# First tile in halves, last tiles by token halves, and three reorderings between them, in a two-block transformer kernel

## The chip, the cores and the metric

One core of a Trainium2 chip runs the kernel. The metric is the device time in microseconds (us) of one launch. TensorE (PE) multiplies, VectorE (DVE) and ScalarE (ACT) work on tiles element by element, GpSimd (POOL) does additions and products, and SyncE (SP) issues every DMA. All tiles are fp32, 128 partitions wide.

## The reference, cut to what matters

Two transformer blocks over 512 tokens of width 1024, then a norm. Cut to what this change touches:

```
# block 1                          # block 2 (same ending, other weights)
u  = rmsnorm(x, g_mix) @ w_in      h = rmsnorm(x1, ln1) @ w_in2   # x1 = rmsnorm(block 1's x, g_fin)
...recurrence, attention...        o_gla  = gated linear attention, o_att = softmax(lse of 3 groups) mix of 12 heads
x += merged @ w_out                mix = (sig(g)*(o_gla*silu(hr))@w_o_gla + sig(g')*o_att@w_o_attn) @ w_out2
x += relu(rmsnorm(x)@w_ff1)**2 @ w_ff2      (the same with w_ml1, w_ml2)
x += sigmoid(rmsnorm(x)@w_pg) * (p@w_ple)   (the same with w_pg2, p_2@w_pp)
                                   y = rmsnorm(x, ln_f)
```

Block 2's first norm is a norm of a norm, so it needs two sums over the width of the squares of block 1's x: a plain one ("n4") and one weighted by g_fin squared ("n5"). The head mix of block 2's attention is a softmax over three group weights for each of 4 heads.

## The kernel before

**Matmuls.** Activations lie transposed, width on partitions, 512 tokens on columns, in 8 row blocks. A weight tile is 128 output columns by 1024 inputs (512 KB). SP loads it into one of 4 buffers RAW, ACT rounds it to fp32r (`whi`, L1106, WHI), DVE makes the remainder (`wlo`, L1658, WLO), in 3 buffers each. A product takes 3 matmuls of 512 columns for each of 8 inner blocks k (`row`, L547 to L549): hi by hi, hi by lo, lo by hi. There are 303 tiles. The activations are split in the same way (`hi` L1137 on ACT, `lo` L1671 or L1669 on DVE).

**Order.** Each engine runs one program in order. It steps through generators woven after one list of rows (`weave_order`); a dense row is the 3 matmuls of one k, so a full tile is 8 rows. The other streams' steps stand ahead of the dense row at which they are put. `due` says at which row of which tile each engine splits or loads a coming tile: ACT at k = 1, DVE at k = 3, SP at k = 5. `lead2(n, skew)` interleaves the rows of a stage's first two tiles.

**Start.** SP loads x block 0, the vectors, weight tile 0, blocks 1 to 3, tile 1, blocks 4 to 7, tile 2, constants, tile 3. Ahead of all weaving, ACT splits the blocks and tiles 0 and 1, then squares 8 blocks (L1121), in turn with POOL's 7 additions (L2323), with two or three buffers between them. Only then does it come to tile 2.

**Norms.** `total` (L568) sums squares over partitions with two ones-matmuls, `norm_rs` takes Ln (L1130) and Exp (L1132) to get RS. An activation function that isn't in the table set that ScalarE holds is preceded by a table load.

**Block 1's gate (pg), then block 2's embedding (emb2).** Per tile i: DVE scales the bank by RS (L1651), ACT sigmoid (L1212), POOL product (L2320), DVE addition into x (L1654), ACT `hi` and square, DVE `lo`, DVE's term of n5 (L1791), POOL's term of n4 (L2323). Both sums take the square as soon as ACT has it. The gate tiles use banks 0 to 3 in turn, and so do the 8 short products of emb2 (2 rows each), which ACT copies out (L1330). Then come n4 and n5, one 16-row tile "ha" and the gla tiles on banks 0 and 1.

**hr stage.** 8 tiles on banks 0 and 1: DVE scales (L1651), ACT sigmoid (L1243), POOL product, DVE product (L1834), ACT hi, DVE lo. In the same rows stream "l" makes the heads' weights on 4 partitions: at row 27 of the stage maximum and difference (L2278), at row 33 two additions, a reciprocal (L2286), a product and three `lo` in one step, and at rows 50, 54, 58 and 62 the mix: 3 small matmuls (L1089) and DVE products each. The stage has 64 rows; the merge of block 2 follows.

**Last gate (pg2) and the end.** Tiles 0 to 6 whole, tile 7 in two token halves of 256 columns. For each half, DVE, ACT, DVE, DVE, ACT (squares L1294, product with ln_f L1296), PE (sums, plain fp32, L649 and L650), ACT (L1300, L1303) and then 8 products (6 on DVE L1651, 2 on POOL) and the stores follow each other.

Of the kernel before, what the change touches and what calls it, by code (L numbers as in the profile page):

```python
# [233 lines left out]
def core_steps():  # L234
# [21 lines left out]
def weave_order():  # L256
# [27 lines left out]
    put("n", A_EMB2 + 8, A_EMB2 + 14, A_HA, *range(A_GL + 1, A_GL + 33, 4))  # L284
# [4 lines left out]
    for n in range(12):  # L289
# [4 lines left out]
    put("l", A_HR + 20, A_HR + 20, A_HR + 20, A_HR + 27, A_HR + 33, *[A_HR + r for r in (50, 54, 58, 62) for _ in range(3)],  # L294
        A_HR + 67)
# [6 lines left out]
def build_kernel(nc, A):  # L302
    ctx = ExitStack()
    with ctx:
# [235 lines left out]
        def tensor_program(e):  # L540
# [31 lines left out]
            def dense():  # L572
# [34 lines left out]
                yield from embed("emb2", T_EMB2, HP2, "HP2")  # L607
# [3 lines left out]
                yield from units(("hr",), T_HR, plain(8), H1, hx("HX2"), ev("hr"), (0, 1))  # L611
# [24 lines left out]
                for half in range(2):  # L636
                    cs = slice(256 * half, 256 * half + 256)
                    b = 4 + half
                    w.wait_ge(D.dve.at("wlo", T_PG2 + 7), free.get(b))
                    for k in range(8):  # L640
                        d = row(bank(b)[:, 0:256], T_PG2 + 7, k, (H3[k][0][:, cs], H3[k][1][:, cs]), k == 0, k == 7)
                        if k == 7:
                            d.then_inc(*D.pe.sig("pg2", 7, half))
                        yield
                for half in range(2):
                    cs = slice(256 * half, 256 * half + 256)
                    acc, tmps = NORM["n8"]
# [2239 lines left out]
```

## Time and profile before

| | us |
|---|---|
| median of 3 runs (lowest, highest) | 2111.76 (2111.15, 2112.51) |
| profiled execution, its own time | 2110.7 |
| its span, first to last instruction | 2108.8 |
| PE busy in it | 2033.7 (96%) |
| DVE, ACT, POOL busy | 990.4, 781.4, 292.6 |

PE is busy for 96% of the span. Its idle time is 75 us, and the profile says for each piece which instruction ended it. The mean granted clock of PE is 0.981 of full speed. Busy times on PE overlap (a matmul is pipelined), so the pace is read from start to start.

### The profile page before, as it was taken

Reading aid. Unit: us, or ns where it says so; the run is one execution under the profiler, and the core shown is the slowest. Engines: PE = TensorE matmul, PEld = TensorE weight load, DVE = VectorE, ACT = ScalarE, POOL = GpSimd, SP = SyncE. Lnnn points to the kernel's source line nnn. Section 1 sums busy time; section 2 is a strip of 40 time slices with the busy share of each in tenths; the row PEclk is TensorE's granted clock in tenths of the full one; section 3 lists DMA queues with packets and bytes.
Section 4 is the critical chain, followed back from the end, with each engine's and each line's share of the span. In section 5 each row is a group of like instructions: output and inputs, shape, how many; then the busy total and the mean of one; then the engine's idle time right before and its main releaser. Section 6 shows DMA issues by size and latency. Waiting matters only on the chain.

```text
span 2108.8 us, 27562 instructions
## 1 busy us (share of the span) xinstructions
PE 2033.7 (96%) x11518; PEld 1629.0 (77%) x11518; DVE 990.4 (47%) x1534; ACT 781.4 (37%) x1233; POOL 292.6 (14%) x292
## 2 busy tenths in 40 slices
PE   7998999999999999999899999998999999999996
PEld 5766767777888778888677788886788888888884
DVE  5665554544553233336855444446643432333354
ACT  5573221223444333234524243335322343322344
POOL 2001121210221001012300000001310220100124
PEclk9999998999999999999999999998999999999997
DMA  5121111111633332322421222221232233322221
GB/s 181 55 70 61 45 48 42 46 47 51 220 100 103 107 103 95 100 93 95 143 90 52 69 71 80 80 90 60 80 100 92 98 125 106 100 98 97 96 80 50
DMA packets 59843, 185.46 MB, mean 88 GB/s; under 512 B 6551, under 2 KB 11799, under 8 KB 59592
## 3 DMA queue, kind: packets, MB, share of 16 engines
q1 hardware_dynamic: 59720, 183.71, 26.2%
q8 instruction: 91, 1.49, 0.3%
q14 instruction: 32, 0.26, 0.0%
HBM read 173.46 MB, written 10.22 MB: 87 GB/s over the span
## 4 chain that ended last, share of the span: by engine, by line
PE 87%; DVE 4%; ACT 4%; issue 2%; POOL 1%; DMA 1%; SPq 0%; DVEq 0%; POOLq 0%; ACTq 0%
PE P L547 25%; PE P L549 24%; PE P L548 24%; DVE AREN L1651 1%; PE P L822 1%; PE P L858 1%; PE P L912 1%; PE P L851 1%; PE P L910 1%; PE P L807 1%; DVE WLO L1658 1%; POOL AREN L2323 1%; DVE AREN L1654 1%; PE P L1035 1%; DVE AREN L1791 1%
## 5 line engine op out<-in xcount | busy, mean ns | idle before, releaser
L547 PE MATMUL P<-HH,WHI 128*128 128x512 f32 x1528 | 624.6, 409 | 22.4 <-DVE WLO L1658 12.2
L549 PE MATMUL P<-HH,WLO 128*128 128x512 f32 x1528 | 603.7, 395 | 0.0
L548 PE MATMUL P<-HL,WHI 128*128 128x512 f32 x1528 | 602.8, 394 | 0.0
L1106 ACT ACTIVATE WHI<-RAW 128x1024 fp32r<-128x1024 f32 x303 | 318.9, 1053 | 443.9 <-PE P L549 440.8
L1658 DVE TENSOR_TENSOR WLO<-RAW,WHI 128x1024 fp32r<-128x1024 f32 x303 | 381.7, 1261 | 150.1 <-ACT WHI L1106 148.8
L547 PEld LDWEIGHTS P<-HH,WHI 128*128 128x128 f32 x1528 | 291.0, 190 | 100.4 <-issue 15.4
L547 PE MATMUL P<-ARR,WHI 128*128 128x512 f32 (+1 forms) x904 | 351.7, 389 | 7.6 <-DVE AREN L1651 2.9
L549 PE MATMUL P<-ARR,WLO 128*128 128x512 f32 (+1 forms) x904 | 350.1, 387 | 0.0
L548 PE MATMUL P<-ARR,WHI 128*128 128x512 f32 (+1 forms) x904 | 350.1, 387 | 0.0
L549 PEld LDWEIGHTS P<-HH,WLO 128*128 128x128 f32 x1528 | 291.1, 190 | 63.3
L548 PEld LDWEIGHTS P<-HL,WHI 128*128 128x128 f32 x1528 | 291.4, 191 | 55.9 <-issue 0.2
L2320 POOL TENSOR_TENSOR AREN<-AREN 128x512 f32<-128x512 f32 (+1 forms) x126 | 132.8, 1060 | 1155.8 <-ACT AREN L1351 560.1
L547 PEld LDWEIGHTS P<-ARR,WHI 128*128 128x128 f32 x904 | 169.7, 188 | 48.1 <-DVE WLO L1658 5.0
L1651 DVE TENSOR_TENSOR AREN<-P,RS 128x512 f32<-128x512 f32 (+1 forms) x136 | 102.2, 752 | 217.0 <-PE P L549 200.6
L549 PEld LDWEIGHTS P<-ARR,WLO 128*128 128x128 f32 x904 | 169.7, 188 | 34.6
L548 PEld LDWEIGHTS P<-ARR,WHI 128*128 128x128 f32 x904 | 169.8, 188 | 34.5
L2323 POOL TENSOR_TENSOR AREN<-AREN 128x512 f32<-128x512 f32 x75 | 117.3, 1564 | 454.6 <-DVE AREN L1651 198.8
L1654 DVE TENSOR_TENSOR AREN<-AREN,P 128x256 f32<-128x256 f32 (+2 forms) x168 | 81.1, 496 | 194.6 <-PE P L549 149.9
L1940 DVE TENSOR_TENSOR ARR<-AREN,ARR 128x512 fp32r<-128x512 f32 x64 | 44.3, 692 | 227.7 <-POOL AREN L2320 211.2
L1351 ACT ACTIVATE AREN<-P 128x512 f32<-128x512 f32 x64 | 38.2, 597 | 200.5 <-PE P L549 200.5
L1651 DVE TENSOR_TENSOR AREN<-AREN 128x256 f32<-128x256 f32 (+1 forms) x80 | 43.3, 560 | 55.8 <-ACT AREN L1402 18.4
L1651 DVE TENSOR_TENSOR AREN<-P,CST 128x256 f32<-128x256 f32 (+3 forms) x80 | 34.4, 447 | 65.8 <-PE P L822 31.5
(297 smaller groups left out, 1553.1 us busy)
## 6 DMA issues: line engine op xcount, KB each, us to landing
RAW<-in_w_in_dram SPq DMA_DIRECT2D x118, 512.0 KB, 3.3
RAW<-in_w_ff_dram SPq DMA_DIRECT2D x64, 512.0 KB, 3.3
RAW<-in_w_ml_dram SPq DMA_DIRECT2D x64, 512.0 KB, 3.2
RAW<-in_w_out_dram SPq DMA_DIRECT2D x16, 512.0 KB, 3.3
RAW<-in_w_pg_dram SPq DMA_DIRECT2D x16, 512.0 KB, 3.3
AREN<-in_xT_dram SPq DMA_DIRECT2D x16, 256.0 KB, 6.4
s_gates<-AREN SPq DMA_DIRECT2D x16, 256.0 KB, 2.0
RAW<-in_w_ab_dram SPq DMA_DIRECT2D x8, 512.0 KB, 3.4
```

The source lines that it names most:

```text
L547: e.matmul(out, hi, H[0][:, s], start=first, stop=False)
L548: e.matmul(out, hi, H[1][:, s], start=False, stop=False)
L549: return e.matmul(out, lo, H[0][:, s], start=False, stop=last)
L807: d = e.matmul(v3(o, 4)[:, 2 * j + p, :], BK[rws[h], j, 2 * p:2 * p + 2, :], AR[rws[h], j, :, p, :], start=True, stop=True)
L1106: e.activation(WHI[n % NSPL][:, :], RAW[n % NRAW][:, :], ACT.Copy).then_inc(*D.act.sig("whi", n))
L1351: e.activation(r, bank((0, 1, 2, 3)[j % 4]), ACT.Relu).then_inc(*D.act.sig(H1, q, j))
L1651: return e.tensor_tensor(out, a, b, ALU.mult)
L1654: return e.tensor_tensor(out, a, b, ALU.add)
L1658: e.tensor_tensor(WLO[n % NSPL][:, :], RAW[n % NRAW][:, :], WHI[n % NSPL][:, :].bitcast(F32), ALU.subtract).then_inc(*D.dve.sig("wlo", n))
L1940: e.tensor_tensor(HD[j][1], ar(19 + u % 3), HD[j][0].bitcast(F32), ALU.subtract).then_inc(*D.dve.sig(f + "D", q, j))
L2320: return e.tensor_tensor(out, a, b, ALU.mult)
L2323: return e.tensor_tensor(out, a, b, ALU.add)
```

## The change

1. *Start.* SP loads the first 512 columns of tile 0 ahead of x block 0, the rest after block 3, tile 1 after block 5, tiles 2 and 3 ahead of the constants; ACT and DVE split tile 0 in two halves. POOL first zeroes a buffer, on which PE runs three plain fp32 matmuls. The first two tiles are interleaved with a skew of 6 rows instead of 2. Of n1's squares, two stay ahead of the weaving and six move into it; POOL adds the first four and DVE the rest; the total goes to bank 2; lambda's small work moves to tiles 3 and 4.
2. *Table sets.* `norm_hi` of n2, n3, n6 and n7 loads the table set that has both Ln and Exp.
3. *n4 and n5.* In the pg stage DVE adds n4 itself; n5's terms (`second`) move to emb2's rows. Squares stay in buffers 30 to 37. emb2 uses banks 4 to 7 and 0 to 3. n4's total is at row 2 of ha (bank 4) and n5's at row 6 (bank 5), instead of row 14 of emb2 and row 0 of ha.
4. *hr.* Four banks instead of two. The weights' steps are at rows 25, 31, 37, 43 and 49, the reciprocal in two halves; the mix is at rows 56, 68, 80 and 92, the last three of which lie in the merge.
5. *End.* Tiles 0 to 4 whole; then tiles 5, 6, 7 for tokens 0 to 255 and again for tokens 256 to 511, so that half 0's sum, its RS and the product of its first 4 blocks on POOL come among half 1's rows. Tile 7's squares are on DVE. The results are written as 4-, 3- and 2-block products on DVE.

```diff
+def last_rows():
+    yield from lead2(5, 0)
+    for u in range(6):
+        for k in range(8):
+            yield 5 + u, k
+def last_steps(j, k):
+    at = {(0, 7): "evac", (1, 0): "sigmoid", (1, 1): "mult", (1, 2): "add", (1, 3): "square", (1, 4): "sum"}
+    return [(5 + u % 3, u // 3, at[j - 5 - u, k]) for u in range(6) if (j - 5 - u, k) in at]
...
-    put("n", A_EMB2 + 8, A_EMB2 + 14, A_HA, *range(A_GL + 1, A_GL + 33, 4))
+    put("n", A_EMB2 + 14, A_HA + 2, A_HA + 6, *range(A_GL + 1, A_GL + 33, 4))
...
-    put("l", A_HR + 20, A_HR + 20, A_HR + 20, A_HR + 27, A_HR + 33, *[A_HR + r for r in (50, 54, 58, 62) for _ in range(3)],
-        A_HR + 67)
+    put("l", A_HR + 20, A_HR + 20, A_HR + 20, *range(A_HR + 25, A_HR + 50, 6),
+        *[A_HR + r for r in (56, 68, 80, 92) for _ in range(3)], A_HR + 97)
...
-                g = units(("attn",), T_AT, lead2(12, 2), H1, hx("HX"), ev("attn"), (0, 1, 6, 7))
+                w.wait_ge(K.pool.at("zero"))
+                for _ in range(3):
+                    e.matmul(bank(3), ar(52)[:, 0:128], ar(52), start=True, stop=True)
+                g = units(("attn",), T_AT, lead2(12, 6), H1, hx("HX"), ev("attn"), (0, 1, 6, 7))
...
-                yield from embed("emb2", T_EMB2, HP2, "HP2")
+                yield from embed("emb2", T_EMB2, HP2, "HP2", (4, 5, 6, 7, 0, 1, 2, 3))
-                yield from units(("hr",), T_HR, plain(8), H1, hx("HX2"), ev("hr"), (0, 1))
+                yield from units(("hr",), T_HR, plain(8), H1, hx("HX2"), ev("hr"), (0, 1, 2, 3))
...
+                for half, banks in ((0, (4, 5, 6)), (1, (1, 2, 3))):
+                    cs = slice(256 * half, 256 * half + 256)
+                    for t, b in zip((5, 6, 7), banks):
+                        w.wait_ge(D.dve.at("wlo", T_PG2 + t), free.get(b))
+                        for k in range(8):
+                            d = row(bank(b)[:, 0:256], T_PG2 + t, k, (H3[k][0][:, cs], H3[k][1][:, cs]), k == 0, k == 7)
+                            if k == 7:
+                                d.then_inc(*D.pe.sig("pg2", t, half))
+                                if half and t == 5:
+                                    last_total(0, 7)
+                            yield
+                last_total(1, 0)
...
             def norm_hi(N_):
+                if N_ not in ("n4", "n5"):
+                    e.preload_act_table_set("natural_log_exp_and_others")
...
                         if at == "lo":
                             lo("HX2", i, hblk(i), xs, g=gl[:, i:i + 1])
-                            w.wait_ge(N.act.at("sq", "n4", i), K.pool.at("gf2"), N.dve.at("n5", i - 1))
...
+                            if i:
+                                w.wait_ge(N.act.at("sq", "n4", i), N.dve.at("n4", i - 1) if i > 1 else None)
+                                add(ar(3), ar(30 if i == 1 else 3), ar(30 + i)).then_inc(*N.dve.sig("n4", i))
+                    for i in [k // 2] if j == 8 and k % 2 == 0 else [4] if (j, k) == (8, 7) else []:
+                        second(i)
...
                 for k in range(8, 16):
                     embed_row(T_EMB2, k)
+                    if k < 11:
+                        second(k - 3)
...
-                e.reciprocal(dZ, dZ).then_inc(*L.dve.sig("zr"))
-                w.wait_ge(L.dve.at("zr"))
+                for half in range(2):
+                    cs = slice(256 * half, 256 * half + 256)
+                    e.reciprocal(dZ[:, cs], dZ[:, cs]).then_inc(*L.dve.sig("zr", half))
+                    yield
+                w.wait_ge(L.dve.at("zr", 1))
                 mul(dL, dL, dZ.unsqueeze(1).to_broadcast([4, 3, 512])).then_inc(*L.dve.sig("lw"))
+                yield
...
             def begin():
+                name, i = TILES[0]
+                load("first", 0, RAW[0][:, 0:512], A[name][i, :, 0:512])
                 for j in range(8):
...
-                    if j in (0, 3, 7):
-                        weights((0, 3, 7).index(j))
+                    if j == 5:
+                        weights(1)
+                    if j == 3:
+                        load("raw0", 0, RAW[0][:, 512:1024], A[name][i, :, 512:1024])
+                weights(2)
+                weights(3)
                 load("cst", 0, CST[:, :], A["consts"])
```

## Rows read from the trace of the kernel before

**Rows 1.** Waits of PE: who waited, for whom: us in total, times, longest.

```profile
PE P L547 <- DVE WLO L1658: 15.1, 8, 9.4
PE P L649 <- ACT AREN L1294: 13.3, 2, 8.0
```

**Rows 2.** Timeline of the start: start, us, engine, line, operation [idle before <-releaser].

```profile
7.00 1.06 ACT L1106 ACTIVATE WHI<-RAW 128x1024 fp32r<-128x1024 f32 x1 [2.33 <-DMA RAW<-in_w_in_dram]
...
9.37 0.80 PE L547 MATMUL P<-HH,WHI 128*128 128x512 f32 x1 [9.37 <-DVE WLO L1658]
...
10.87 1.06 ACT L1106 ACTIVATE WHI<-RAW 128x1024 fp32r<-128x1024 f32 x1 [0.57 <-DMA RAW<-in_w_in_dram]
...
12.10 0.63 PE L547 MATMUL P<-HH,WHI 128*128 128x512 f32 x1
...
12.52 0.63 PE L548 MATMUL P<-HL,WHI 128*128 128x512 f32 x1
...
14.69 0.43 PE L547 MATMUL P<-HH,WHI 128*128 128x512 f32 x1
...
15.50 10.86 POOL L2323 TENSOR_TENSOR AREN<-AREN 128x512 f32<-128x512 f32 x7 [10.82 <-ACT AREN L1121]
...
25.27 0.50 PE L547 MATMUL P<-HH,WHI 128*128 128x512 f32 x1 [2.21 <-DVE WLO L1658]
...
32.35 0.47 PE L547 MATMUL P<-HH,WHI 128*128 128x512 f32 x1 [0.87 <-ACT RS L1130]
```

**Rows 3.** Timeline from gate to gla: PE, DVE, ACT.

```profile
995.48 1.28 ACT L1132 ACT_TABLE_LOAD   x1
...
999.39 0.50 PE L547 MATMUL P<-ARR,WHI 128*128 128x512 f32 x1 [0.46 <-DVE WLO L1658]
...
1020.75 2.31 DVE L1658 TENSOR_TENSOR WLO<-RAW,WHI 128x1024 fp32r<-128x1024 f32 x1
...
1025.45 1.78 DVE L1791 SCALAR_TENSOR_TENSOR AREN<-AREN,GF 128x512 f32<-128x512 f32 x1
...
1030.86 0.75 DVE L1671 SCALAR_TENSOR_TENSOR HL<-AREN,DVC,HH 128x512 fp32r<-128x512 f32 x1 [0.19 <-ACT HH L1137]
...
1036.79 0.50 PE L547 MATMUL P<-ARR,WHI 128*128 128x512 f32 x1 [2.90 <-DVE AREN L1651]
...
1056.16 0.47 PE L547 MATMUL P<-HH,WHI 128*128 128x512 f32 x1 [1.61 <-DVE AREN L1651]
```

**Rows 4.** Timeline of hr: DVE, PE.

```profile
1456.56 3.34 DVE L2286 RECIPROCAL AREN<-AREN 4x512 f32<-4x512 f32 x1
...
1462.51 0.39 PE L549 MATMUL P<-HH,WLO 128*128 128x512 f32 x1
...
1470.60 0.77 PE L547 MATMUL P<-HH,WHI 128*128 128x512 f32 x1 [7.71 <-DVE AREN L1651]
...
1483.63 0.50 PE L547 MATMUL P<-HH,WHI 128*128 128x512 f32 x1
```

**Rows 5.** Stretch of 10 us in hr: us, busy (x) of PE, PEld, DVE, ACT, POOL, PE clock, DMA.

```profile
1470.00:1480.00 10.00, 9.40 (x21) 6.56 (x22) 8.07 (x10) 2.85 (x5) 5.14 (x4) 0.50 0.22 61
```

**Rows 6.** Timeline of the end.

```profile
2058.93 1.76 DVE L1654 TENSOR_TENSOR AREN<-AREN 128x512 f32<-128x512 f32 x1 [1.18 <-POOL AREN L2320]
...
2065.05 0.39 PE L547 MATMUL P<-ARR,WHI 128*128 128x512 f32 x1
...
2065.73 0.39 PE L547 MATMUL P<-ARR,WHI 128*128 128x512 f32 x1
...
2083.61 0.28 PE L549 MATMUL P<-ARR,WLO 128*128 128x256 f32 x1
...
2085.76 0.42 DVE L1651 TENSOR_TENSOR AREN<-P,RS 128x256 f32<-128x256 f32 x1
...
2099.22 1.22 PE L649 MATMUL P<-AREN,CST 128*128 128x256 f32 x2 [7.99 <-ACT AREN L1294]
...
2102.29 3.16 DVE L1651 TENSOR_TENSOR AREN<-AREN 128x256 f32<-128x256 f32 x6 [3.93 <-ACT AREN L1303]
```

More of the change, by code:

```diff
@@ L635, in dense, with last_total @@
                     yield
-                for half in range(2):
+                for half, banks in ((0, (4, 5, 6)), (1, (1, 2, 3))):
                     cs = slice(256 * half, 256 * half + 256)
[L638 to L647, printed above, removed]
-                    w.wait_ge(N.pool.at("add", "n8", 6), N.act.at("sq", "n8", 7 + half), free.get(6 + half))
-                    e.matmul(bank(6 + half)[:, 0:256], cst("ones"), ar(acc)[:, cs], start=True, stop=False)
-                    e.matmul(bank(6 + half)[:, 0:256], cst("ones"), ar(tmps[(7 + half) % 2])[:, cs], start=False,
-                             stop=True).then_inc(*N.pe.sig("sum", "n8", half))
+                    for t, b in zip((5, 6, 7), banks):
[8 more added lines that the diff above has]
+                last_total(1, 0)
+            def last_total(half, b):
+                cs = slice(256 * half, 256 * half + 256)
+                acc, tmps = NORM["n8"]
+                w.wait_ge(N.pool.at("add", "n8", 6, half), K.pool.at("one"), free.get(b))
+                e.matmul(bank(b)[:, 0:256], cst("ones"), ar(acc)[:, cs], start=True, stop=False)
+                w.wait_ge(N.dve.at("sq", "n8", 7, half))
+                e.matmul(bank(b)[:, 0:256], cst("ones"), ar(tmps[1])[:, cs], start=False,
+                         stop=True).then_inc(*N.pe.sig("sum", "n8", half))
             def block(t_out, out, HM_, hm, emb, t_emb, HP_, hp, f, t_ml, n2, pg, t_pg, n3, h3):
@@ L1305, in whi_mg2, with last_rs @@
+            def last_rs(half, b):
+                rs = ar(6)[:, 256 * half:256 * half + 256]
+                w.wait_ge(N.pe.at("sum", "n8", half))
+                e.activation(rs, bank(b)[:, 0:256], ACT.Ln, scale=1.0 / 1024, bias=EPS6).then_inc(
+                    *N.act.sig("ln", "n8", half))
+                w.wait_ge(N.act.at("ln", "n8", half))
+                e.activation(rs, rs, ACT.Exp, scale=-0.5).then_inc(*N.act.sig("rs", "n8", half))
             def whi_mg2(i, k):
@@ L2511, in dilated @@
                         yield
-                for _ in range(5):
+                for _ in range(8):
                     yield
```

287 lines of the change are left out of this document (170 added, 117 removed).

## The prediction

> **What bounds the kernel now.** I read PE's waits first. The two longest kinds, 15.1 us for `wlo` and 13.3 us for ScalarE's squares [rows 1], lie with few others in five stretches; outside them PE is fed without a break, and a row of three matmuls takes 0.68 us from start to start (2065.05 to 2065.73) [rows 6], a tile 5.44 us. So only what shortens an idle stretch of PE, or the work behind its last matmul, is worth anything. Then I read the timeline of each stretch. In the start the reader is to see that PE begins at 9.37, that its matmuls come 0.42 us apart (12.10, 12.52) until 14.69, and that ScalarE's and GpSimd's alternation on n1 (10.86 us) keeps tile 2 from being split [rows 2]. From gate to gla, that VectorE is what PE waits for [rows 3]. In hr, that one scaling behind the reciprocal stops PE, and that the clock is at half for some 13 us behind the stop [rows 4, 5]. At the end, that 25 us follow PE's last tile [rows 6].
>
> **Part 1, the start.** Before, 16 rows of the first two tiles, tile 2 (24 matmuls) and n1's total end such that tile 3 starts at 32.35 [rows 2]. After: tile 0 landed by 7.00, when 0.85 MB were issued ahead of and with it; tile 1 by 10.87, at 2.16 MB; that is 340 KB per us [rows 2]. In the new order tile 1 ends at 2.68 MB, so it lands near 10.87 + 0.52/0.34 = 12.4. Blocks 6 and 7 follow, 0.26 MB each: 13.2 and 14.0. With ACT's split of tile 1 (1.06), VectorE's (1.2), then `hi` (0.7) and `lo` (0.75 [rows 3]), row 6 can start near 15.2. The six rows of tile 0 ahead of it (8 us at the slow pace, from near 7) fit before. The ten left are 6.8 us: both tiles end at 22. Tile 2 is split by then, since only two squares stand before it (ACT free near 16, split at 18). It takes 5.44, the total 0.5, and the total's bank no longer holds tile 3 (0.87 [rows 2]): tile 3 starts near 28.3 instead of 32.35. Gain 4.0. The three plain fp32 matmuls lie before the first load has landed; if they cost more than that, up to 1 us of row 0, it is before the data-bound rows. Bounds: 6.8 us of the ten rows become 12.8 where they run at the slow pace, gain -2; tile 1 landing at 11, gain 5.4.
>
> **Part 2, the table sets.** In pg and pg2 a table load of 1.28 stands between Ln and Exp [rows 3], and one ahead of Ln: RS comes some 2.5 us sooner. Tile 3 then doesn't wait (0.46 and 0.3 of refilling the pipe [rows 3]): 0.75 in each of the two stages, counted in parts 3 and 5. In the two MLPs no wait hangs on RS: 0.
>
> **Part 3, gate to gla.** From tile 3's start at 999.39 to gla's at 1056.16 [rows 3] there are 196 matmuls (5 tiles 120, emb2 48, totals 4, ha 24), 44.4 us at the full pace; 56.8 were taken. VectorE per gate tile had `wlo` 2.31, `lo` 0.75, n5's term 1.78, addition and scaling 0.68 each: 6.2 us against 5.44. The 2.31 (elsewhere 1.23) and the 1.78 (0.75 for the like `lo`) overlap with GpSimd's additions of n4 [rows 3]. After it: 1.23 + 0.75 + 4 x 0.68 less one, 4.0, and at most 1.1 for GpSimd's product (an addition of 0.68 took 1.76 beside one [rows 6]): 5.1, under PE's 5.44. So the gate tiles run at PE's pace, and end at 998.65 + 27.2 = 1025.9. Eight banks take away the waits of emb2 (2.90 for the last scaling [rows 3], 1.8 for the copies): it ends at 1036.8. What is late next is n4. The scaling of tile 7 comes some 2.5 us behind PE at 1028.4, as the chain from RS through product and addition to the next scaling lags; behind it stand on VectorE the rest of the last two tiles, eight terms of n5 and two `wlo`, 12.4 us: n4's `lo` ends near 1041. PE is at ha's row 2 at 1038.2 and waits 2.7. Four rows and the second total later it is 1044.6, then product 0.7, Ln and Exp 1.4, RS 0.7 and ha's scaling 0.7 (bank 0, which gla's first tile needs): gla starts at 1048.1. Gain 56.16 - 48.1 = 8.0, the 0.75 of part 2 in it. Bounds: no wait left but ha's, 10.5; n5's terms at 1.78 instead of 0.75, which is 8 us more of VectorE, 1.5. I take 8.0, as GpSimd has nothing to do in emb2's rows.
>
> **Part 4, hr.** PE's fifth tile ends at 1462.74 (the last start is 1462.51), the next starts at 1470.60; from there to 1483.63 are 18 matmuls and two mix groups [rows 4], at half clock (0.50 [rows 5]). At full pace these are 18 x 0.2265 + 2 x 1.8 = 7.7 us of the 13.0. The stop and the slow clock cost 7.9 + 5.3 = 13.2. After: VectorE's chain in these rows doesn't get shorter, but two scalings more may be late. I count it from the end T of tile 2 (1446.4 before): difference 4.9, `wlo` and product 6.7; additions and half a reciprocal (3.34/2 [rows 4]) 9.8; tile 3 scaled 11.1; `wlo`, the other half, product, `lo`, tile 4 scaled 16.9; product of the weights and `wlo` of tile 7 19.9; tile 5 scaled 22.7; the weights' three `lo` 23.3, 24.0, 24.6. PE needs bank 3 at T + 27 and `wlo` of tile 7 at T + 21.8: no wait. But the mix at row 56 comes at T + 21.8 and wants the weights at 23.3 to 24.6: PE idles some 1.9, and a stop of 2.90 left the next matmuls at their full pace in part 3's stretch, so no clock is lost. The nine other mix products lie beside the merge, whose first need for the mix is row 112, 15 rows (10 us) behind the last step. Gain 13.2 - 2.2 = 11.0. Bounds: each of the four long VectorE steps 1.1 later for GpSimd's product, with the clock falling again, 5; no wait, 13.2.
>
> **Part 5, the end.** Before, tile 7 ends at 2083.9 and the span at 2108.8 [rows 6]. After, tiles 0 to 4 end at 2066.3 (0.75 sooner). Each half tile is 24 matmuls of 0.12: 2.9 us. Half 0 ends at 2075, half 1's tile 5 at 2077.8. VectorE lags here too (it scales tile 7's half 0 at 2085.76, 4.9 us behind PE [rows 6]); with RS 2.5 sooner, tile 5 half 0 is scaled near 2072.7, and each half tile takes scaling 0.42, sigmoid 0.4, product 0.45, addition 0.42, square and product 0.8, 2.3 to 2.5 in all: tile 7's square on VectorE ends at 2079.8. PE waits 1.5 for it, the sum ends at 2080.35, half 1's tiles end at 2083.2 and 2086.1. RS of half 0 is at 2081.3, then a table load 1.28 ahead of tile 5's sigmoid at 2082.6. GpSimd's product of 1024 columns takes some 2.6 (2 x 1.3) from there; VectorE's product of tile 5 is behind it and comes at 2084.4. From there each half tile is 2.3 again: last addition 2089.2, square 2089.6, PE 2090.2 to 2090.7 (slow), Ln and Exp 2091.6, results 0.9, 0.9 and 0.7: 2094.1, and 3.3 for the last store, as before (2102.29 + 3.16 to 2108.8): 2097.3. Gain 11.5. Bounds: a lag as large as before and all contended operations at 1.76 instead of 0.68 (some four on the chain), 7; half 1 free of GpSimd and PE's clock full, 13.
>
> A row first: VectorE's addition beside GpSimd's product took 1.76 instead of 0.68 [rows 6], that is, about to the end of that product. The Trainium skill (SBUF — State Buffer, "Who interferes with whom") says that the two share a port pair which one holds for a whole instruction, and that the other fully blocks. By that the one long product on GpSimd can hold VectorE for its whole 2.6 us, where four short ones would let it in between: it speaks against this piece of the change, the end would be near 2098.5, and the total 1.2 later.
>
> **Sum.** 4.0 + 8.0 + 11.0 + 11.5 = 34.5 us. The profiled execution took 2110.7 for a span of 2108.8; the median is 2111.8, 1.1 above. 2111.8 - 34.5 = 2077.3; I say 2078.
>
> **Rivals.**
> *A, the weights come later than PE in hr.* VectorE is in order, and four long steps stand among its eight tiles; for it speaks that it was busy 8.1 of 10 us there [rows 5], against it that four banks give 16 us of slack. PE would stop some 6 us at row 56, with a slow clock behind it: gain there 3, total 2086.
> *B, the end keeps its length.* The half tiles' chain lags as tile 7 did; PE then waits 4 us for half 0's sum and the rest moves with it: gain 7, total 2082.
> *C, the start runs at the slow clock.* PE has pauses between the first six rows, where it had none: gain -2 in part 1, total 2084.
> *D, the other side: the slow clock lasts.* Rows are 1.28 us at half clock, tiles 10.2 instead of 5.44 [rows 2, 6], 4.8 us lost each. A start with pauses, or the pause in hr, would have to hold it for 8 tiles (35 + 4 us) for the kernel to be slower by over 0.2%; at nine it is 2120. Against it: the clock was back some 5 us after 9.37 and 13 us after 1470.60.
> *E, nothing changes.* It would need VectorE's load in emb2's rows and in hr to give all back; no row says so.
>
> **Chances and range.** My forecast, within 4 us: 45%; A 17%, B 14%, C 11%, a better one (all stops gone, 2071) 9%, D 3%, E 1%. The range 2070 to 2089 takes in A to C with their neighbours and leaves out some 15%. A difference of 0.2%, 4.2 us, is about what can be told from none: faster 0.95, same 0.02, slower 0.03.
>
> **What would show it.** Tile 3 starts near 28 and no wait for `wlo` near 22; fp32 matmuls before the first load. Between gate and gla, `wlo` at 1.23, one wait of 2 to 3 us for n4's `lo` and one of 2 for ha's scaling. In hr one wait below 3 us ahead of the mix and a clock of 1.00. At the end less than 12 us between PE's last fp32r matmul and the last instruction. A wait of over 3 us ahead of the mix, or ahead of half 0's sum, or matmuls 0.42 us apart for most of the first 25 us, proves me wrong there.

## The result and the profile after

The changed kernel takes 2089.73 us (median of four executions, 2086.41 to 2093.19), the kernel before on the same chip 2111.45 (2109.63 to 2112.51): a ratio of 0.9911, 95% interval 0.9885 to 0.9937. It is 21.7 us faster. The prediction was 2078 with a range of 2070 to 2089, so the time lies 0.7 us outside it, which is less than the 6.8 us by which the four executions differ. The direction was right, and more than a third of the forecast gain is missing.

The profiled execution took 2090.74 for a span of 2089.0 (before 2110.7 and 2108.8). To see where the time went I cut both spans at the same weight tiles: a stage lasts from the start of VectorE's `wlo` of one tile to that of another, so a stage means the same work in every kernel. The cuts after are at 60.21, 952.17, 1110.21, 1393.03, 1550.64 and 2033.12.

| us | before | after | gained | predicted |
|---|---|---|---|---|
| start | 64.60 | 60.21 | 4.4 | 4.0 |
| recurrence and first half of block 1 | 892.40 | 891.96 | 0.4 | 0 |
| gate to gla | 159.69 | 158.04 | 1.65 | 8.0 |
| dil | 282.80 | 282.82 | 0.0 | 0 |
| hr and merge | 161.26 | 157.61 | 3.65 | 11.0 |
| out2 and second MLP | 482.48 | 482.48 | 0.0 | 0 |
| end | 65.57 | 55.88 | 9.7 | 11.5 |

Start and end came as forecast or nearly so; of the 19 us forecast for the two stages in the middle, 5.3 arrived. The waits of PE, which for the kernel before were led by 15.1 and 13.3 us for `wlo` and the squares [rows 1], now read so (who waited, for whom: us in total, times, longest):

```profile
PE P L1116 <- DVE ARR L2396: 5.9, 2, 5.7
PE P L675 <- POOL AREN L2428: 4.3, 2, 2.5
...
PE P L561 <- ACT AREN L1382: 2.6, 1, 2.6
...
PE P L561 <- DVE WLO L1712: 1.8, 1, 1.8
```

L561 to L563 are a row's three matmuls (L547 to L549 before), L1712 is `wlo`, L1705 a product or scaling. The waits for `wlo` are down to 1.8 (one wait at 535.5, outside the five stretches) and those of the last sums to 4.3 on L675 and 1.2 on L677, as forecast in kind. The longest single wait is now the 5.7 us for L2396, the weights' `lo` of the heads' mix.

**The start.** Timeline of the kernel after (start, us, engine, line, operation, idle before and releaser), which answers to [rows 2]:

```profile
1.31 4.33 PE L595 MATMUL P<-AREN 128*128 128x512 f32 x6 [1.31 <-POOL DVC L2439]
...
6.57 0.47 PE L561 MATMUL P<-HH,WHI 128*128 128x512 f32 x1 [0.93 <-DVE HL L1725]
...
14.64 0.50 PE L561 MATMUL P<-HH,WHI 128*128 128x512 f32 x1 [1.68 <-DVE HL L1725]
...
27.49 0.40 PE L561 MATMUL P<-HH,WHI 128*128 128x512 f32 x1
```

Six rows of tile 0 run from 6.57, PE is fed without a break from 14.64 (forecast: row 6 near 15.2), no wait for `wlo` is left near 22, and tile 3 starts at 27.49 behind n1's total without a wait (forecast 28.3; before 32.35).

**Gate to gla.** Timeline, which answers to [rows 3]:

```profile
1026.72 0.57 ACT L1382 ACTIVATE AREN<-P 128x512 f32<-128x512 f32 x1
...
1032.12 1.06 ACT L1382 ACTIVATE AREN<-P 128x512 f32<-128x512 f32 x2
...
1034.02 1.57 ACT L1382 ACTIVATE AREN<-P 128x512 f32<-128x512 f32 x3
...
1034.76 0.47 PE L561 MATMUL P<-HH,WHI 128*128 128x512 f32 x1 [2.58 <-ACT AREN L1382]
...
1037.95 0.68 DVE L1732 TENSOR_TENSOR ARR<-AREN,ARR 128x512 fp32r<-128x512 f32 x1
...
1038.69 0.79 PE L584 MATMUL P<-ARR,ONES 128*128 128x512 f32 x1 [1.39 <-DVE ARR L1732]
...
1048.03 0.47 PE L561 MATMUL P<-HH,WHI 128*128 128x512 f32 x1 [2.51 <-DVE AREN L1705]
```

and its stretches of 5 us (busy time and count of PE, PEld, DVE, ACT, POOL, then PE's granted clock, DMA share, GB/s):

```profile
1030.00:1035.00 5.00, 2.42 (x11) 1.75 (x10) 4.80 (x8) 4.03 (x8) 0.00 (x0) 1.00 0.71 262
1035.00:1040.00 5.00, 3.61 (x9) 2.36 (x9) 4.93 (x8) 3.58 (x8) 0.00 (x0) 0.52 0.48 138
```

The gate tiles and the embedding run at PE's pace: emb2 ends at 1034.76 - 2.58 = 1032.18, which is 38.1 us behind tile 3's start near 994.1, just the 27.2 and 10.9 us that were counted. Then come three waits, 2.58 + 1.39 + 2.51, of which only the last two were foreseen. The first is for ScalarE's copies of emb2's products (L1382): they stand in order behind the last gate tile, six of the eight come after 1032, and ha writes bank 0, which holds the fifth product (the first of the three copies from 1034.02). Behind the first wait the granted clock is near half (0.52).

**hr.** Timeline and stretches, which answer to [rows 4, 5]:

```profile
1442.16 1.75 DVE L2379 TENSOR_TENSOR AREN<-AREN 4x1536 f32<-4x1536 f32 x1
...
1443.94 1.49 ACT L1674 ACTIVATE AREN<-AREN 4x1536 f32<-4x1536 f32 x1 [3.94 <-DVE AREN L2379]
...
1446.41 1.23 DVE L1712 TENSOR_TENSOR WLO<-RAW,WHI 128x1024 fp32r<-128x1024 f32 x1 [2.50 <-ACT WHI L1133]
...
1447.69 0.63 ACT L1283 ACTIVATE AREN<-AREN 128x512 f32<-128x512 f32 x1
...
1449.72 0.75 DVE L1910 SCALAR_TENSOR_TENSOR AREN<-AREN,VEC 128x512 f32<-128x512 f32 x1 [2.08 <-POOL AREN L2425]
...
1454.02 0.67 DVE L1705 TENSOR_TENSOR AREN<-P,RS 128x512 f32<-128x512 f32 x1
...
1466.79 2.97 DVE L2396 TENSOR_TENSOR ARR<-AREN,ARR 4x512 fp32r<-4x512 f32 x3
...
1467.52 2.07 PE L1116 MATMUL P<-ARR,EYE 4*128 4x512 f32 x4 [5.66 <-DVE ARR L2396]
```

```profile
1465.00:1470.00 5.00, 2.25 (x5) 1.33 (x6) 4.42 (x6) 2.05 (x3) 1.61 (x1) 0.53 0.08 32
1470.00:1475.00 5.00, 5.00 (x12) 3.48 (x13) 4.23 (x7) 2.21 (x3) 0.64 (x1) 0.50 0.30 105
```

PE comes to the mix at 1467.52 - 5.66 = 1461.86, the forecast T + 21.8 with T = 1440.0 for the end of tile 2. The first of the weights' three `lo` is ready at T + 27.5 instead of T + 23.3. Look at VectorE's two idle times, 2.50 and 2.08: it waits there for ScalarE (L1133), and then for GpSimd, whose product waits for ScalarE's sigmoid (L1283); and ScalarE stood idle 3.94 for VectorE's L2379. The two wait for each other in turn.

**The end.** Timeline, which answers to [rows 6]:

```profile
2060.09 2.14 POOL L2428 TENSOR_TENSOR AREN<-AREN 128x512 f32<-128x512 f32 x1 [1.47 <-ACT AREN L1147]
...
2063.51 0.69 DVE L1708 TENSOR_TENSOR AREN<-AREN 128x512 f32<-128x512 f32 x1 [2.43 <-POOL AREN L2425]
...
2070.35 0.70 PE L675 MATMUL P<-AREN,CST 128*128 128x256 f32 x2 [2.45 <-POOL AREN L2428]
...
2073.37 2.40 POOL L2425 TENSOR_TENSOR AREN<-AREN 128x1024 f32<-128x1024 f32 x1 [3.07 <-ACT AREN L1354]
...
2075.05 0.99 DVE L1705 TENSOR_TENSOR AREN<-AREN 128x256 f32<-128x256 f32 x1 [3.14 <-ACT AREN L1338]
...
2082.86 2.43 DVE L1705 TENSOR_TENSOR AREN<-AREN 128x768 f32<-128x768 f32 x3 [0.61 <-ACT AREN L1354]
```

PE's last fp32r tile ends near 2078.1 (the wait of 1.81 for the second sum begins there), 10.9 us before the span's end; before it was 25 us.

### The profile page after: what moved, and what is told of

Read it like the earlier page. It is cut to its first block, busy times and chain, and to the rows that moved or that the text cites. A ratio compares the mean times of both kernels' runs of the same rounds, so it can differ in the third digit from the quotient of the medians.

```text
span 2089.0 us, 27641 instructions
## 1 busy us (share of the span) xinstructions
PE 2033.5 (97%) x11572; PEld 1631.0 (78%) x11572; DVE 983.1 (47%) x1549; ACT 775.4 (37%) x1233; POOL 278.3 (13%) x279
## 4 chain that ended last, share of the span: by engine, by line
PE 88%; DVE 4%; ACT 4%; issue 2%; POOL 1%; DMA 1%; SPq 0%; DVEq 0%; POOLq 0%; ACTq 0%
PE P L561 25%; PE P L563 24%; PE P L562 24%; DVE AREN L1705 1%; PE P L849 1%; PE P L885 1%; POOL AREN L2425 1%; PE P L939 1%; DVE AREN L1708 1%; PE P L878 1%; PE P L937 1%; PE P L834 1%; ACT WHI L1133 1%; PE P L1062 1%; PE P L1028 1%
## 5 line engine op out<-in xcount | busy, mean ns | idle before, releaser
L561 PE MATMUL P<-HH,WHI 128*128 128x512 f32 x1528 | 623.0, 408 | 10.7 <-DVE HL L1725 3.8
L563 PE MATMUL P<-HH,WLO 128*128 128x512 f32 x1528 | 602.2, 394 | 0.0
L1133 ACT ACTIVATE WHI<-RAW 128x1024 fp32r<-128x1024 f32 x302 | 317.9, 1053 | 438.3 <-PE P L563 437.5
L1712 DVE TENSOR_TENSOR WLO<-RAW,WHI 128x1024 fp32r<-128x1024 f32 x302 | 374.8, 1242 | 144.6 <-ACT WHI L1133 143.1
L561 PEld LDWEIGHTS P<-HH,WHI 128*128 128x128 f32 x1528 | 289.9, 190 | 89.0 <-issue 15.9
L561 PE MATMUL P<-ARR,WHI 128*128 128x512 f32 (+1 forms) x920 | 353.8, 385 | 0.0
L563 PE MATMUL P<-ARR,WLO 128*128 128x512 f32 (+1 forms) x920 | 352.9, 384 | 0.0
L563 PEld LDWEIGHTS P<-HH,WLO 128*128 128x128 f32 x1528 | 290.3, 190 | 63.1
L2425 POOL TENSOR_TENSOR AREN<-AREN 128x512 f32<-128x512 f32 (+2 forms) x121 | 130.3, 1083 | 1146.3 <-ACT AREN L1403 561.2
L561 PEld LDWEIGHTS P<-ARR,WHI 128*128 128x128 f32 x920 | 172.9, 188 | 36.8 <-issue 3.0
L1705 DVE TENSOR_TENSOR AREN<-P,RS 128x512 f32<-128x512 f32 (+1 forms) x138 | 102.4, 743 | 206.6 <-PE P L563 196.0
L563 PEld LDWEIGHTS P<-ARR,WLO 128*128 128x128 f32 x920 | 172.9, 188 | 34.1
L562 PEld LDWEIGHTS P<-ARR,WHI 128*128 128x128 f32 x920 | 172.9, 188 | 34.0
L2428 POOL TENSOR_TENSOR AREN<-AREN 128x512 f32<-128x512 f32 (+1 forms) x66 | 102.9, 1560 | 430.2 <-DVE AREN L1705 194.1
L1705 DVE TENSOR_TENSOR AREN<-AREN 128x256 f32<-128x256 f32 (+3 forms) x78 | 43.7, 572 | 54.7 <-ACT AREN L1454 18.4
L1705 DVE TENSOR_TENSOR AREN<-P,CST 128x256 f32<-128x256 f32 (+3 forms) x80 | 34.6, 447 | 64.8 <-PE P L849 32.9
```

What stands on the lines that cost most here:

```text
L561: e.matmul(out, hi, H[0][:, s], start=first, stop=False)
L562: e.matmul(out, hi, H[1][:, s], start=False, stop=False)
L563: return e.matmul(out, lo, H[0][:, s], start=False, stop=last)
L1133: e.activation(WHI[n % NSPL][:, :], RAW[n % NRAW][:, :], ACT.Copy).then_inc(*D.act.sig("whi", n))
L1705: return e.tensor_tensor(out, a, b, ALU.mult)
L1712: e.tensor_tensor(WLO[n % NSPL][:, :], RAW[n % NRAW][:, :], WHI[n % NSPL][:, :].bitcast(F32), ALU.subtract).then_inc(*D.dve.sig("wlo", n))
```

## The experiments

Each kernel is the changed one but for the lines of its diff. Stages are cut as above. Stages that an edit doesn't touch repeat from kernel to kernel within 0.9 us, with two exceptions: the recurrence (see the last section), and gate to gla, which is 156.5 in five such profiles and 158.0 and 158.4 in two. So an edit is judged by its own stage. Where no range is given with a time, the kernel was executed once.

**The changed kernel once more**, to know how far its stages repeat.

> The changed kernel itself, beside the next one on the same chip and against the kernel before. The three runs that had its recurrence unchanged show that part, from row marks in the trace, at 886 to 894 us for the same instructions, with different stretches of half clock in each. Theory: this, not the change, is why whole times scatter by several us; the stages outside it come out again as start 60, gate to gla 156.5 to 158, hr 157.6, end 55.9 to 56.7 us (marks as before: 64.6, 159.7, 161.3, 65.6), so the change is worth 19 to 20 us, 0.9905 of before. Rival: the stages scatter as much as the whole; then these marks move by over 2 us.

Measured: 2090.05 (2083.92 to 2092.73, six executions), ratio 0.9912 (0.9891 to 0.9933). Start 60.24, gate to gla 156.51, hr 157.37, end 56.58, recurrence 894.62. In the middle stage PE's three waits are there again (2.60, 2.30, 2.49), but ha's first rows run at full clock. So the 158.04 of the first profile has 1.5 us that come from a slow clock in that execution, and the usual gain of this stage is 3.2 us.

**hr: VectorE's first step two rows later.**

```
-        put("l", ..., *range(A_HR + 25, A_HR + 50, 6),
+        put("l", ..., A_HR + 27, *range(A_HR + 31, A_HR + 50, 6),
```

> The changed kernel with the first step of the heads' weights (maximum, difference, and ScalarE's exponential) at row 27 of hr instead of row 25, as it was before the change; all else as changed. Theory: at row 25 the step stands ahead of ScalarE's split of the next weight tile and of its sigmoid, so that both wait for VectorE's difference (the exponential started at 1443.94, the sigmoid only at 1447.69), and VectorE then waits 2.5 and 2.1 us for them; this is what makes the weights late at row 56. Then the sigmoid comes before the exponential, VectorE's two waits shrink to under 1 us together, the stop of PE at row 56 falls from 5.66 to 1 to 3 us, and the half clock behind it goes away: 3 to 6 us off the changed kernel, about 2085. Rival: VectorE simply has too much to do in these rows (the long steps and GpSimd's products beside them); then the stop stays above 4.5 us and the time within 1 us.

Measured: 2084.89 (2078.55 to 2084.99), ratio 0.9896 (0.9867 to 0.9925). The stage takes 153.99 instead of 157.6, and the wait ahead of the mix, 5.66 and then 0.23 before, is down to (VectorE's and PE's timeline in that kernel):

```profile
1442.60 1.21 DVE L1712 TENSOR_TENSOR WLO<-RAW,WHI 128x1024 fp32r<-128x1024 f32 x1
1443.74 0.73 DVE L1910 SCALAR_TENSOR_TENSOR AREN<-AREN,VEC 128x512 f32<-128x512 f32 x1
...
1461.56 1.32 PE L1116 MATMUL P<-ARR,EYE 4*128 4x512 f32 x4 [1.92 <-DVE ARR L2396]
1463.87 1.22 PE L1116 MATMUL P<-ARR,EYE 4*128 4x512 f32 x2 [1.00 <-DVE ARR L2396]
```

Nothing was taken from VectorE; only the order changed, so that `whi` and the sigmoid of the next tile no longer stand on ScalarE behind an Exp that waits for VectorE. VectorE's idle times of 2.50 and 2.08 ahead of `wlo` and of its product are gone. That 5.66 + 0.23 became 1.92 + 1.00 shows that the chain's order, and not VectorE's load, made half of the stop. The theory held. The whole times don't tell this kernel from the changed one (their intervals overlap), the stage does.

**hr: the mix four rows later**, VectorE's order as in the changed kernel.

```
-        *[A_HR + r for r in (56, 68, 80, 92) for _ in range(3)], A_HR + 97)
+        *[A_HR + r for r in (60, 72, 84, 96) for _ in range(3)], A_HR + 101)
```

> The other part of the combination alone: the mix products stand at rows 60, 72, 84 and 96 and the last step at 101, instead of 56, 68, 80, 92 and 97; VectorE's first step stays at row 25. Theory: the weights' lo is ready when it was, PE has 4 rows (2.7 us) more of work ahead of it, so the stop of 5.66 us shrinks to about 2.9, and the stage from 157.6 to 154.9 or, if a shorter stop also shortens the half clock behind it, as low as 153. Row 27 and these rows together gave 148.6, 9.0 less; row 27 alone 3.6. Rival: the stop moves with the product, because something behind it in VectorE's order (not the weights) holds PE, and the stage stays within 1 us of 157.6.

Measured: 2083.88, stage 155.14 (expected 154.9). The stop is spread over three waits, 3.65 us in all:

```profile
1457.85 0.50 PE L561 MATMUL P<-HH,WHI 128*128 128x512 f32 x1 [1.10 <-DVE WLO L1712]
1462.44 1.32 PE L1116 MATMUL P<-ARR,EYE 4*128 4x512 f32 x4 [1.57 <-DVE ARR L2396]
1464.74 1.22 PE L1116 MATMUL P<-ARR,EYE 4*128 4x512 f32 x2 [0.98 <-DVE ARR L2396]
```

The stage is as expected and the rival is out, but the stop didn't simply shrink: a part of it is now a wait for tile 7's `wlo`, which stands in the same chain of VectorE. Moving PE's step (2.5 us gained) or moving VectorE's (3.6) each cures a part. Behind the stop the clock is still at 0.50 (1465 to 1470).

**Gate to gla: ha in bank 6** instead of 0, so that it doesn't wait for the copy of the fifth product.

```
-                yield from units(("ha",), T_HA, plain(1), H1, hx("HX2"), ev("ha"), (0, 1))
+                yield from units(("ha",), T_HA, plain(1), H1, hx("HX2"), ev("ha"), (6, 7))
```

> The changed kernel with tile ha on bank 6 instead of bank 0; all else as changed. Theory: ha waits 2.58 us only because its bank holds the fifth product of emb2, which ScalarE copies out late (it is in order behind the last gate tile), and gla's first tile waits 2.51 us only because ha's scaling, at the end of the chain of n4 and n5, holds bank 0. With bank 6 both waits go. But n4's total stands in ha's rows, and n4's remainder is ready only near 1038.6, so PE then waits some 4 us there instead of 1.4: of 6.5 us of stops 4 stay, and gla starts 2 to 3 us sooner, at 1045 to 1046 of this trace; the clock may still fall once. Rival: the stops don't matter, the chain n4, n5, RS sets gla; then gla starts at 1047 to 1048 as now.

Measured: 2084.71 (2080.59 to 2089.12), ratio 0.9896 (0.9861 to 0.9932); the stage takes 153.69 instead of 156.5. Two waits instead of three, and none ahead of gla, since gla's first bank is free:

```profile
1035.29 0.47 PE L561 MATMUL P<-HH,WHI 128*128 128x512 f32 x1 [0.67 <-ACT AREN L1382]
1041.14 0.51 PE L584 MATMUL P<-ARR,ONES 128*128 128x512 f32 x1 [4.22 <-DVE ARR L1732]
```

The time saved at the bank (1.9) was given to n4's `lo`, where PE now waits longer; what was truly gained is the wait of 2.5 ahead of gla. The theory held but for 0.67 us of waiting that is left at the bank.

**Gate to gla: the two totals at rows 6 and 7 of ha**, bank 0 as in the changed kernel.

```
-    put("n", A_EMB2 + 14, A_HA + 2, A_HA + 6, ...
+    put("n", A_EMB2 + 14, A_HA + 6, A_HA + 7, ...
```

> One part of the earlier combination alone: the two totals of n4 and n5 stand at rows 6 and 7 of ha instead of 2 and 6; ha's bank stays 0. In the changed kernel PE waits 2.58 us ahead of ha for ScalarE's fifth copy, 1.39 for n4's lo, 2.51 for ha's scaling, and has half clock behind the first and around the last. Theory: the first wait stays, since it hangs on the bank, the second goes, since four rows (2.7 us) stand ahead of it; the last stays near 2.5 and with it the stretch of slow clock. Gate to gla 156.5 less 1.4 = 155.1 (154.3 to 155.8), so that the bank and the rows together (150.6 in the combination, 5.9 less) are worth more than the bank alone (2.8) and the rows alone (1.4) added. Rival: the worth of the two simply adds, and this kernel comes to 153.3. The whole time 2089 give or take 5 for the recurrence.

Measured: 2079.40, stage 156.44. I had expected 155.1 for the stage and 2089 for the whole, give or take 5. The whole is 4.6 us under that because the recurrence took 881.77 in this execution. The stage's rows:

```profile
1029.20 0.40 PE L584 MATMUL P<-ARR,ONES 128*128 128x512 f32 x1
...
1031.25 0.50 PE L584 MATMUL P<-ARR,ONES 128*128 128x512 f32 x1 [0.72 <-DVE ARR L1732]
1035.85 0.77 PE L561 MATMUL P<-HH,WHI 128*128 128x512 f32 x1 [3.19 <-DVE AREN L1705]
```

n4's total, at 1029.20, waits no longer, as expected. The 0.72 at 1031.25 is for the `lo` of n5, which now stands behind a `wlo` on VectorE. In all PE waits 6.5 us instead of 7.4, and gla's first tile starts 93.45 us into the stage instead of the 94.3 of three kernels that don't touch this stage (it is 95.9 to 96.2 in four, whose clock fell sooner). So the rows alone bring gla 0.9 us forward. The stage is no shorter all the same, since the wait ahead of gla is 3.19 instead of 2.5 and the clock behind it is at 0.50 (1035 to 1040; 0.71 over the 10 us from 1030).

**Three moves together**: row 27, the mix at rows 60 to 96, ha in bank 6 with the totals at rows 6 and 7.

> The changed kernel with three moves and nothing else: the first step of the heads' weights at row 27; the mix at rows 60, 72, 84 and 96 with the last step at 101; tile ha on bank 6 with n4's total at row 6 and n5's at row 7 of ha. Theory: what failed were orders, not loads. In gate to gla, bank 6 alone took that stage from 156.5 to 153.7 and left 4.22 us of waiting for n4's remainder at row 2; four rows later that wait is under 2 us and the clock stays full: 150 to 152. In hr, row 27 alone took the stage from 157.6 to 154.0 and left stops of 1.92 and 1.00 us; four rows later no stop is left and no half clock behind it: 151 to 152.5. Together 9 to 12 us under the changed kernel. Rival: VectorE is the bound in both; the waits only move behind (ahead of gla's first tiles, and into the merge), and the two stages gain under 1.5 us each over bank 6 and row 27 alone.

Measured: 2077.67 (2073.23 to 2078.59, five executions), ratio to the kernel before 0.985 (0.9827 to 0.9874), 12.4 us under the changed kernel on the same chip. Gate to gla takes 150.59, hr 148.60. The longest wait of each stage and the clock around it (PE's starts, then stretches of 10 us):

```profile
1041.34 0.50 PE L584 MATMUL P<-ARR,ONES 128*128 128x512 f32 x1 [1.48 <-DVE ARR L1732]
...
1461.29 0.73 PE L1116 MATMUL P<-ARR,EYE 4*128 4x512 f32 x2 [0.41 <-DVE ARR L2396]
```

```profile
1040.00:1050.00 10.00, 7.77 (x33) 6.10 (x34) 7.54 (x11) 6.09 (x9) 0.00 (x0) 1.00 0.48 157
...
1460.00:1470.00 10.00, 9.59 (x41) 7.34 (x40) 8.46 (x11) 3.51 (x5) 2.23 (x2) 1.00 0.29 105
```

The theory held, and both stages came out a little better than expected. The parts don't add: bank and rows alone gave 2.8 and 0.0, together 5.9; row 27 and the mix rows alone gave 3.6 and 2.5, together 9.0. Each part alone leaves a wait behind which the clock falls (over 5 us to 0.72 with the bank, 0.50 with the totals' rows, 0.52 with row 27, 0.50 with the mix rows); together no wait over 1.48 is left in the two stages, and the clock is 1.00 throughout both. An estimate for hr adds PE's stops to its busy time times what the clock lacks of 1.00, by stretches of 5 us: 9.7 us in the changed kernel, 5.8 with row 27, 6.8 with the mix rows, 0.4 with both. That gives gains of 3.9, 2.9 and 9.3 where 3.6, 2.5 and 9.0 were measured, so stops and clock together make up nearly all of the difference. In hr that makes 161.26 - 148.60 = 12.7 us against the kernel before, near the upper bound of part 4 (13.2); between gate and gla 9.1, past the 8.0 of part 3. So the forecast gains were there to be had; the change as made doesn't reach them.

**Without the table set ahead of the statistics.**

```
-                if N_ not in ("n4", "n5"):
-                    e.preload_act_table_set("natural_log_exp_and_others")
```

> The changed kernel without its choice of the table set that has both Ln and Exp (in the norms n2, n3, n6 and n7). Theory: a load of 1.28 us stands again between Ln and Exp and one ahead of Ln; RS comes 2.5 us later in both gates, tile 3 waits again for its remainder (0.46 us and the refill), and the lag of the gate chain behind PE grows: the stage gate to gla gets 0.7 to 2.5 us longer, and the end 0.7 to 2.5. Rival: the lag is made good before it matters; both stages stay within 0.4 us.

Measured: 2098.36; gate to gla 159.92, 3.4 us more than the usual 156.5, and end 60.00, 3.3 to 4.2 more than in the others. Both are past the 0.7 to 2.5 that I had expected. ScalarE without it, in the first of the two stages (the line numbers are 2 lower in this kernel):

```profile
990.54 1.28 ACT L1156 ACT_TABLE_LOAD   x1
...
992.55 1.28 ACT L1158 ACT_TABLE_LOAD   x1
...
1039.19 0.77 PE L561 MATMUL P<-HH,WHI 128*128 128x512 f32 x1 [4.36 <-ACT AREN L1380]
```

Two loads of 1.28 stand in the path of RS. PE loses only 0.46 to that at tile 3, but the chain of the gate tiles starts 2.6 later and stays late to its end: ha waits 4.36 instead of 2.6 and starts 2.5 us later in the stage. The rest of the 3.4 comes behind that wait, where the clock is at 0.50 and 0.64 for 10 us. Against the two profiles whose clock fell there too (158.0 and 158.4) the difference is 1.5 to 1.9, so in this stage a single execution gives the table set a worth of 1.5 to 3.4.

**Without the three fp32 matmuls at the start.**

```
-                w.wait_ge(K.pool.at("zero"))
-                for _ in range(3):
-                    e.matmul(bank(3), ar(52)[:, 0:128], ar(52), start=True, stop=True)
```

> The changed kernel without the three plain fp32 matmuls at the start (they compute nothing that is used). Theory: they are what has PE at the full clock from its first row at 6.57. Without them the matmuls stand 0.42 us apart at least for the six rows of tile 0 and into the ten rows from 14.64; these ten then take up to 3 us more than 6.8, and tile 3 starts up to 3 us later. Rival: the start is bound by the loads and the splits alone; then the ten rows still begin at 14.6, run 0.23 us apart, and tile 3 starts at the same time within 0.3 us.

Measured: 2087.41, start 60.53 (with them 60.04 to 60.63 in ten profiles). The rival held. PE's first rows are then slow (0.63 us a matmul until 9.5, 0.39 from 10.48 on), and it makes no difference (line numbers here are 3 lower):

```profile
6.29 0.76 PE L561 MATMUL P<-HH,WHI 128*128 128x512 f32 x1 [6.29 <-DVE HL L1722]
...
14.95 0.51 PE L561 MATMUL P<-HH,WHI 128*128 128x512 f32 x1 [1.71 <-DVE HL L1722]
```

The six first rows wait for their data whatever their pace, and behind 14.95 the clock is full in both. Which of the start's other pieces (loads, halves, skew, squares) gives how much of the 4.4 wasn't tested.

**The end: half 0's sum one tile later**, and **GpSimd's product in four pieces of 256 columns** (with the waits of what reads it set to match).

```
-                                if half and t == 5:
+                                if half and t == 6:
```

> The changed kernel with the sum of half 0 on PE behind tile 6 of half 1 instead of behind its tile 5; nothing moved on the other engines. PE waits 2.45 and 0.58 us for that sum now. Theory: half 1 is bound by the chain on ScalarE and VectorE that begins with half 0's RS and the table load, and tile 7 is scaled 0.4 us after PE ends it only by chance; with the sum later PE's wait goes almost wholly, but the sum itself comes at the same time, and the stretch from the last whole tile to the last instruction gets shorter by 0 to 0.5 us. Rival: PE's stop is carried to the end; then that stretch gets shorter by 2.5 to 3 us.

```
-                        y = v3(ar(8, 8), 8)[:, 0:4, 0:256]
-                        w.wait_ge(N.act.at("rs", "n8", 0), *[D.act.at("xg", i) for i in range(4)])
-                        mul(y, y, ar(6)[:, 0:256].unsqueeze(1).to_broadcast([128, 4, 256])).then_inc(*D.pool.sig("y"))
+                        for i in range(4):
+                            w.wait_ge(N.act.at("rs", "n8", 0), D.act.at("xg", i))
+                            mul(ar(8 + i)[:, 0:256], ar(8 + i)[:, 0:256], ar(6)[:, 0:256]).then_inc(*D.pool.sig("y", i))
```

> The changed kernel with GpSimd's product of four blocks of half 0 as four instructions of 256 columns in place of one of 1024; nothing else. Now the one instruction runs from 2073.37 for 2.40 us, and VectorE's product of 256 columns beside it took 0.99 instead of 0.42. Theory (one engine holds the shared way to SBUF for a whole instruction): VectorE gets in after the short instruction that runs, its product takes 0.45 to 0.8, and the end is up to 0.5 us shorter. Rival: with four instructions VectorE meets GpSimd more often and the end is the same or up to 0.6 us longer.

Measured: 2083.13 with end 56.34, and 2082.69 with end 56.04, against 55.83 to 56.72 in the kernels that don't touch it: neither is worth anything that shows. With the sum later PE's wait for it is 0.45 instead of 2.45 + 0.58, and the next sum waits 4.68 instead of 1.81, and its two pairs of matmuls then take 1.22 us instead of 0.70, which is 0.5 us more in the chain to the end. PE's stop of 3 us is hidden, since the chain of the half tiles on VectorE and ScalarE sets the end. Of the four pieces:

```profile
2065.13 3.01 POOL L2425 TENSOR_TENSOR AREN<-AREN 128x256 f32<-128x256 f32 x4 [3.08 <-ACT AREN L1354]
2066.82 0.72 DVE L1705 TENSOR_TENSOR AREN<-AREN 128x256 f32<-128x256 f32 x1 [3.15 <-ACT AREN L1338]
2067.57 0.85 DVE L1708 TENSOR_TENSOR AREN<-AREN 128x256 f32<-128x256 f32 x1
```

They take 3.01 instead of 2.40, and hold VectorE twice (0.72 and 0.85 for operations of 0.42) where the long one holds it once (0.99). The Trainium skill (SBUF — State Buffer, "Who interferes with whom") calls the port pair that the two engines share an exclusive lock. That the other engine fully blocks it says of VectorE's 2-port modes; of a VectorE instruction with two SBUF inputs, as this product is, it says that it contends with GpSimd's reads. The traces agree and show a full block here: VectorE's product ends 0.27 us behind GpSimd's long instruction, and 0.28 behind a piece in both cases with four. But the piecewise form, which the prediction held to be the better one by that rule, comes out even. GpSimd is ahead of VectorE by 1.7 us when their work meets, so little of the long instruction is left to wait for.

## Why the prediction was right and wrong

**Part 1, the start: right**, 4.4 against 4.0. The data bound it and the rows took the places given (its terms, 15.2 + 6.8 + 5.44 + 0.5, add to 27.9 and not to 28.3; measured 27.49). The warm matmuls, costed at nothing, are worth nothing.

**Part 2, the table sets: mis-sized.** The prediction put it at 0.75 in each stage, the wait at tile 3; the run without it shows 1.5 to 3.4 in the one and 3.3 to 4.2 in the other. RS comes 2.6 us sooner, and the whole chain of scalings behind it keeps that lead up to ha and to the end. Parts 3 and 5 started their chains from the sooner RS, so the sum has most of this under their names: the wait at tile 3 was only the smaller way in which RS acts. Of the 9.7 us gained at the end, 3.3 to 4.2 hang on it.

**Part 3, gate to gla: the step that failed is "Eight banks take away the waits of emb2 ... What is late next is n4".** Emb2's own waits are gone and it ends on time. But the next user of the ring is ha, whose bank 0 holds the fifth product, and ScalarE copies that only behind the last gate tile: 2.58 us that I hadn't counted. Bank 6 shows it (0.67 left). The second miss is n4's `lo`: measured from tile 3's start it came 2.2 us later than counted. VectorE was busy 4.80 and 4.93 of 5 us, as assumed, but took up the last gate tile 0.7 later than counted and then waited 1.0 for ScalarE's sigmoid, which stood behind the first copy of emb2. The third is the clock: the prediction had none lost, and between n4's `lo` and the end of the second total 5.5 us passed instead of 3.6. The wait ahead of gla was foreseen at 2 and is 2.5. One reading came right for another reason than the one given: `wlo` did fall from 2.31 to 1.23, but before it stood beside GpSimd's product (1020.41 to 1021.98) and not beside the addition of n4, and that product is still there. Now `wlo` starts first (1021.48 against 1022.04), and it is the product that takes 1.82 instead of 1.28. The usual gain of this stage is 3.2 (1.65 in the profile of the table), against 8.0.

**Part 4, hr: the step that failed is VectorE's chain, "tile 3 scaled 11.1".** Each of its steps was counted back to back from VectorE's durations alone. The chain passes twice through ScalarE: Exp waits for VectorE's difference, `whi` and the sigmoid of the next tile wait for Exp, and a table load of 1.28 stands between. Up to VectorE's difference the count was even late (T + 3.9 measured, 4.9 counted); then the two waits for ScalarE and for what hangs on it, 2.50 and 2.08, put the product at T + 10.5 instead of 6.7. The scaling of tile 3 ended at T + 14.7 instead of 11.1, that of tile 4 at T + 20.1 instead of 16.9, that of tile 5 at T + 26.9 instead of 22.7, and the three `lo` took 2.97 beside a product on GpSimd instead of 1.88. The stop was 5.66 instead of 1.9, and half clock followed it (0.53, 0.50). That is rival A, with its own figures: a stop of some 6 us, gain 3, total 2086; it had 17%. Moving one step by two rows took 3.0 us off the stops (5.9 to 2.9), with VectorE's work the same. What the four banks are worth by themselves wasn't tested.

**Part 5, the end: mechanism right, size 1.8 too large.** The half tiles' chain was some 1.3 us later than counted (tile 5's half scaled 7.7 us behind the end of tile 4, where 6.4 were counted), because GpSimd's addition took 2.14 beside VectorE's `wlo` and its product and VectorE's addition came behind it. PE's wait for half 0's sum was 3.0 instead of 1.5 to 2 and cost nothing of its own. VectorE's product beside the long one took 0.99, not the 2.4 that would have made the end 1.2 longer.

**The other rivals.** B, the end keeps its length: no, it is 9 to 10 us shorter. C, the start at the slow clock: no, a matmul behind a row's first takes 0.40 us from the first row on (0.63 before [rows 2]). D, a slow clock that lasts for eight tiles: no; after the stop of 5.66 us it lasted some 8 us, to 1475. E: no.

The range missed because parts 3 and 4 failed together: they fell short by 6.4 and 7.4 us, and part 5 added 1.8. Each alone was in the range (A gives 2086), but their common ground, that a chain over two engines was costed by one engine's durations, makes them one risk, and they were treated as two.

## What to carry to other kernels

A chain that goes to and fro between two in-order engines is to be counted on both queues at once: for each step write down what stands ahead of it on its own engine, and when that was released. When a ring of buffers is made larger, look at the next user of the ring: it meets the same late reader. And several short waits close together are best removed together: in both stages here the parts alone gave less than the whole, because behind the wait that was left the clock still fell.

## What the runs showed of the hardware

The scatter of the whole time, 2084 to 2093 for one and the same kernel, comes from the recurrence: that stage took 881.8 to 894.6 us with its instructions unchanged, while the other stages hardly move. In some stretches of it the clock is granted only in part though PE is busy throughout, and which stretches these are differs between executions. Two stretches of 10 us, first of the changed kernel, then of the one with the totals at rows 6 and 7:

```profile
380.00:390.00 10.00, 10.00 (x77) 7.36 (x76) 4.57 (x11) 0.46 (x1) 3.22 (x6) 0.50 0.07 28
```

```profile
480.00:490.00 10.00, 10.00 (x79) 7.79 (x79) 1.54 (x3) 2.33 (x7) 0.00 (x0) 0.66 0.07 28
```

In the second kernel the stretch from 380 to 390 is at 1.00 and in the first the one from 480 to 490 at 0.95. The clock makes up most of the scatter. Multiply each stretch of 10 us from 60 to 950 by what its clock lacks of 1.00, and add them up: the sum is 18.8 us in the changed kernel and 8.5 in that other one, 10.3 less, and the stage took 891.96 and 881.77 us, 10.2 less. Less this sum the stage takes 872 to 875 us in all twelve profiles, that of the kernel before (20.4 us) included. What decides when such stretches come no run here shows. A stop's length doesn't settle either whether the clock falls: a wait of 2.90 left the next matmuls at full pace before [rows 3], and of two executions of the changed kernel one had near half clock behind its wait of 2.58 (0.52) and the other full clock behind the same wait, 2.60 there.
